# Second-type FFN of a twelve-part transformer program: two wide matmuls per product in place of three, all up products ahead of the down products

## The reference

```
def swiglu(x, w_gu, w_down):
    g, u = jnp.split(x @ w_gu, 2, axis=-1)
    return (jax.nn.silu(g) * u) @ w_down

h = x + 0.5 * swiglu(rmsnorm_2(x, g[0]), w_ffn_gu[layer, 0], w_ffn_down[layer, 0])
xn = rmsnorm_2(h, g[1])
...                                  # one of three mixers on xn, added to h
h = h + 0.5 * swiglu(rmsnorm_2(h, g[2]), w_ffn_gu[layer, 1], w_ffn_down[layer, 1])
gate = jax.nn.sigmoid(rmsnorm_2(h, g[3]) @ w_ple_gate[layer])
x = h + gate * (p[layer] @ w_ple_proj[layer])
```

## Time and profile before

| | us |
|---|---|
| median of three runs | 3411.81 (3410.1 to 3412.32) |
| span of the profiled execution, first to last instruction | 3410.7 |
| PE busy | 3235.4 (95%) |
| DVE busy | 2467.3 (72%) |
| ACT busy | 1768.7 (52%) |
| mean granted clock of TensorE, share of full | 0.968 |

### The profile page before, as it was taken

One profiled execution on the slowest core, in us unless ns is written; L12 is line 12 of the kernel. 1 busy time (PEld: TensorE's weight loads), 2 busy tenths in 40 slices (PEclk: granted clock), 3 DMA queues, 4 the chain that ended last, 5 costly groups with the idle time before them and its releaser, 6 DMA issues.

```text
span 3410.7 us, 64690 instructions
## 1 busy us (share of the span) xinstructions
PE 3235.4 (95%) x27210; PEld 3128.6 (92%) x27210; DVE 2467.3 (72%) x3720; ACT 1768.7 (52%) x2677; POOL 3.0 (0%) x6
## 2 busy tenths in 40 slices
PE   6899999999999999979999997999999999997999
PEld 6789899988989999879999987999989999997899
DVE  8987699887767766876676656667676667678666
ACT  4556444556554554665454535455455455457544
POOL 0000000000000000000000000000000000000000
PEclk8899999989999999989999998999999999998999
DMA  8455488434546555425555533555543555552453
GB/s 303 141 175 192 151 317 305 152 129 142 185 155 217 171 187 188 153 92 184 188 178 190 187 116 124 190 180 185 188 147 127 186 184 183 190 173 88 153 190 125
DMA packets 164353, 597.95 MB, mean 175 GB/s; under 512 B 18240, under 2 KB 18272, under 8 KB 163936
## 3 DMA queue, kind: packets, MB, share of 16 engines
q1 hardware_dynamic: 164064, 593.81, 51.5%
HBM read 592.69 MB, written 1.05 MB: 174 GB/s over the span
## 4 chain that ended last, share of the span: by engine, by line
PE 81%; DVE 12%; ACT 5%; issue 1%; DMA 1%; SPq 0%; DVEq 0%; ACTq 0%
PE ps L458 26%; PE ps L460 25%; PE ps L459 25%; DVE wlo L418 3%; ACT whi L406 1%; DVE fa L1527 1%; PE ps L1119 1%; ACT hh L1723 1%; DVE hl L1761 1%; PE ps L1235 0%; DVE land L533 0%; DMA land<-w_ada 0%; DVE fa L2225 0%; DMA land<-w_in 0%; DVE tmps L1801 0%
## 5 line engine op out<-in xcount | busy, mean ns | idle before, releaser
L458 PE MATMUL ps<-hh,whi 128*128 128x256 f32 x5472 | 1546.9, 283 | 46.7 <-DVE hl L732 20.5
L459 PE MATMUL ps<-hl,whi 128*128 128x256 f32 x5472 | 1536.2, 281 | 0.0
L460 PE MATMUL ps<-hh,wlo 128*128 128x256 f32 x5472 | 1535.6, 281 | 0.0
L418 DVE TENSOR_TENSOR wlo<-land,whi 128x1024 fp32r<-128x1024 f32 (+1 forms) x1032 | 1216.5, 1217 | 192.3 <-ACT whi L406 191.4
L406 ACT ACTIVATE whi<-land 128x1024 fp32r<-128x1024 f32 (+1 forms) x1032 | 1029.2, 1046 | 150.4 <-PE ps L460 136.1
L458 PEld LDWEIGHTS ps<-hh,whi 128*128 128x128 f32 x5472 | 1037.3, 190 | 56.2 <-issue 36.1
L459 PEld LDWEIGHTS ps<-hl,whi 128*128 128x128 f32 x5472 | 1037.3, 190 | 0.7
L460 PEld LDWEIGHTS ps<-hh,wlo 128*128 128x128 f32 x5472 | 1036.7, 189 | 0.0
L458 PE MATMUL ps<-ra,whi 128*128 128x256 f32 (+1 forms) x2416 | 684.3, 283 | 21.6 <-DVE ra L1435 11.9
L459 PE MATMUL ps<-ra,whi 128*128 128x256 f32 (+1 forms) x2416 | 679.4, 281 | 0.0
L460 PE MATMUL ps<-ra,wlo 128*128 128x256 f32 (+1 forms) x2416 | 679.1, 281 | 0.0
(11 more groups left out here) (416 smaller groups left out, 2441.9 us busy)
## 6 DMA issues: line engine op xcount, KB each, us to landing
land<-w_gu SPq DMA_DIRECT2D x352, 512.0 KB, 3.5
land<-w_dn SPq DMA_DIRECT2D x176, 512.0 KB, 3.5
land<-w_in SPq DMA_DIRECT2D x136, 512.0 KB, 3.8
land<-w_ada SPq DMA_DIRECT2D x96, 512.0 KB, 3.7
land<-w_up SPq DMA_DIRECT2D x88, 512.0 KB, 4.2
land<-hg_in SPq DMA_DIRECT2D x64, 512.0 KB, 3.5
land<-w_down SPq DMA_DIRECT2D x44, 512.0 KB, 4.5
land<-ple_gate SPq DMA_DIRECT2D x32, 512.0 KB, 3.5
```

The lines of the kernel that those rows point to most:

```text
L418: dve.tensor_tensor(w.lo, g.slot(n), w.hi.bitcast(F32), ALU.subtract).then_inc(*D_("w_lo", n))
L458: pe.matmul(out, w.hi, x.hi, start=first, stop=False, skip_group_check=skip)
L459: pe.matmul(out, w.hi, x.lo, start=False, stop=False, skip_group_check=skip)
L460: return pe.matmul(out, w.lo, x.hi, start=False, stop=last, skip_group_check=skip)
```

## The change

Only the second-type FFN changes, besides the layout of buffers. The hi and lo parts of h and of the inner activation now lie in one buffer at a fixed distance (class `Operand`, with `both` for the two), so that a unit is two matmuls (`wide`): w.lo·x.hi over 256 columns into the left half of a bank, and w.hi on both parts of x over 512 columns into both halves. A product so takes a whole bank, and its left and right halves have to be added by whoever reads it.

- The 22 up products come first, each in two banks (`up_banks`: 0 and 1, 2 and 3, 4 and 5, 6 and 7 in turn), and their activations are all kept (`y`, 128x11264, hi and lo). Then the down product is made chunk by chunk of the output, bank m for chunk m, over all 22 inner chunks; the down weights are laid out in that order on the host (`halved`).
- Per j, ScalarE copies the right halves of both banks (`up_right`, new, 128x512), VectorE adds them to the left halves (`up_read`, new, 128x512) and then multiplies by the factor (`up`). The splits of two tiles stand between these steps.
- The additions to x are made during the down product, two banks at a time, each in two instructions (left, right), and with them the next stage's hi parts, squares and lo parts for chunks 0 to 5; chunk 6 is added at tile 19, and chunk 7 (part 4) after the last tile.
- `norm2_tensor` stays after j = 1.

The diff, cut to the second-type FFN:

```diff
+def wide(pe, ps, w, x, first, last):
+    pe.matmul(ps[:, 0:T], w.lo, x.hi, start=first, stop=False, skip_group_check=True)
+    return pe.matmul(v2(ps), w.hi, x.both, start=False, stop=last, skip_group_check=True)
...
+    if before[0] == "h":
+        added_halves_vector(g, dve, before, ffn_number(before), 4)
+        for k in halves(3):
+            rest_vector(g, dve, st, which, k)
+        pair_vector(g, dve, st, 3)
+        reduced_vector(g, dve, st)
+        return
...
+def up_banks(j):
+    return 2 * (j % 4), 2 * (j % 4) + 1
+def up_tensor(g, pe, st, i, j, ready=None):
+    a, b = up_banks(j)
+    n = [take_tensor(g, pe, "w_gu", half) for half in halves(i * 22 + j)]
+    for bank in (a, b):
+        pe.wait_ge(*W(*g.banks.use(bank, "up_read", st, j)))
+    for k, c in [(k, c) for k in range(8) for c in range(2)] if ready else [(k, c) for c in range(2) for k in range(8)]:
+        if ready and c == 0:
+            pe.wait_ge(*W(*ready[k]))
+        mm = wide(pe, g.ps[(a, b)[c]], g.weights(n[c])[:, k * 128:(k + 1) * 128], g.h.chunk(k), k == 0, k == 7)
+        if k == 7:
+            mm.then_inc(*D_("tile", n[c]))
+def down_banks_tensor(g, pe, st, i, y):
+    for t in range(NF):
+        n = take_tensor(g, pe, "w_dn", down_tile(i, t))
+        for b in range(8):
+            m, k = divmod(8 * t + b, NF)
+            if m == 0:
+                pe.wait_ge(*W("inner", st, k))
+            if k == 0:
+                pe.wait_ge(*W(*g.banks.use(m, *(("acc_read", st, 3) if m == 6 else ("x", AFTER[st], m // 2)))))
+            mm = wide(pe, g.ps[m], g.weights(n)[:, b * 128:(b + 1) * 128], y.chunk(k), k == 0, k == NF - 1)
+            if b == 7:
+                mm.then_inc(*D_("tile", n))
+            elif k == NF - 1 and m in (1, 3, 5, 6):
+                mm.then_inc(*D_("acc", st, m))
...
 def second_ffn_tensor(g, pe, st, i):
     second_norm_tensor(g, pe, st)
-    ffn_tensor(g, pe, st, "w_gu", i * 22, "w_dn", i * 11, inner_pairs(g.ra2))
+    y = inner_operand(g)
+    up_tensor(g, pe, st, i, 0, chunks("h", st))
+    for p in range(NF // 2):
+        for j in halves(p):
+            if j:
+                up_tensor(g, pe, st, i, j)
+        if p == 0:
+            norm2_tensor(g, pe, st)
+    down_banks_tensor(g, pe, st, i, y)
...
+        act.wait_ge(*W("tile", n))
+        act.activation(v2(c), halves_of_banks(g, up_banks(j)[0], 2)[:, :, 1, :], ACT.Copy).then_inc(*D_("up_right", st, j))
+        if j > 1:
+            catch_up_scalar(g, act, n, 1)
+        act.wait_ge(*W("up", st, j))
         act.activation(b[:, 0:T], a[:, 0:T], ACT.Silu).then_inc(*D_("silu", st, j))
+        if j > 1:
+            catch_up_scalar(g, act, n)
         act.wait_ge(*W("prod", st, j))
...
+    for t in range(NF):
+        take_scalar(g, act, "w_dn", down_tile(i, t))
+        if t in (6, 12, 17):
+            q = (6, 12, 17).index(t)
+            gained_scalar(g, act, nx, next_norm(i), q)
+            square_scalar(g, act, nx, q)
...
 def second_ffn_vector(g, dve, st, i):
     D_, W = g.m.done, g.m.when
     second_norm_vector(g, dve, st, i // 2 * 4 + i % 2 * 2)
-    R = inner_pairs(g.ra2)
+    y, nx = inner_operand(g), AFTER[st]
     r = g.small[:, T:2 * T]
     for j in range(NF):
         p = j // 2
-        if j != 1:
-            take_vector(g, dve, "w_gu", *halves(i * 22 + j))
         if j == 0:
+            take_vector(g, dve, "w_gu", *halves(i * 22))
             take_vector(g, dve, "w_gu", *halves(i * 22 + 1))
             factor_vector(g, dve, st)
+        elif j > 1:
+            take_vector(g, dve, "w_gu", *halves(i * 22 + j), behind=2)
         n = g.index["w_gu", 2 * (i * 22 + j) + 1]
         if j == 10 and st[1] == "b":
-            low_vector(g, dve, ("p", "pl" + st[2]), ple_operand(g), g.fa2[:, 4096:4608], ("p_hi", "pl" + st[2]))
-        a, b = g.t(j % 2), g.t(2 + j % 2)
-        dve.wait_ge(*W("tile", n))
-        dve.tensor_tensor(v2(a), v2(g.ps[4 + j % 3][:, :]), bc2(r), ALU.mult).then_inc(*D_("up_read", st, j))
+            low_vector(g, dve, ("p", "pl" + st[2]), ple_operand(g), per_layer(g), ("p_hi", "pl" + st[2]))
+        a, b, c = g.t(j % 2), g.t(2 + j % 2), g.t(4 + j % 2)
+        dve.wait_ge(*W("up_right", st, j))
+        dve.tensor_tensor(v2(a), halves_of_banks(g, up_banks(j)[0], 2)[:, :, 0, :], v2(c), ALU.add).then_inc(
+            *D_("up_read", st, j))
+        dve.wait_ge(*W("up_read", st, j))
+        dve.tensor_tensor(v2(a), v2(a), bc2(r), ALU.mult).then_inc(*D_("up", st, j))
+        if j > 1:
+            catch_up_vector(g, dve, n, 1)
         dve.wait_ge(*W("silu", st, j))
-        dve.wait_ge(*W("up_read", st, j))
+        dve.wait_ge(*W("up", st, j))
         dve.tensor_tensor(b[:, T:2 * T], b[:, 0:T], a[:, T:2 * T], ALU.mult).then_inc(*D_("prod", st, j))
-        low_vector(g, dve, ("inner", st, j), R[p % 3].chunk(j % 2), b[:, T:2 * T], ("inner_hi", st, j))
-        if j % 2 and p:
-            take_vector(g, dve, "w_dn", *halves(i * 11 + p - 1))
-    take_vector(g, dve, "w_dn", *halves(i * 11 + NF // 2 - 1))
+        if j > 1:
+            catch_up_vector(g, dve, n)
+        low_vector(g, dve, ("inner", st, j), y.chunk(j), b[:, T:2 * T], ("inner_hi", st, j))
+    for t in range(NF):
+        take_vector(g, dve, "w_dn", down_tile(i, t))
+        if t in (5, 11, 16):
+            added_halves_vector(g, dve, st, i, (5, 11, 16).index(t))
+        elif t in (6, 12, 17):
+            q = (6, 12, 17).index(t)
+            for k in halves(q):
+                rest_vector(g, dve, nx, next_norm(i), k)
+            if q:
+                pair_vector(g, dve, nx, q)
+        elif t == 19:
+            added_halves_vector(g, dve, st, i, 3)
+def added_halves_vector(g, dve, st, i, part):
+    first, n = ((0, 2), (2, 2), (4, 2), (6, 1), (7, 1))[part]
+    s, banks = g.x[:, first * T:(first + n) * T].rearrange("p (b t) -> p b t", b=n), halves_of_banks(g, first, n)
+    dve.wait_ge(*W(*acc_ready(g, st, i, part)))
+    dve.scalar_tensor_tensor(s, banks[:, :, 0, :], 0.5, s, ALU.mult, ALU.add).then_inc(*D_("acc_left", st, part))
+    dve.wait_ge(*W("acc_left", st, part))
+    dve.scalar_tensor_tensor(s, banks[:, :, 1, :], 0.5, s, ALU.mult, ALU.add).then_inc(
+        *(D_("acc_read", st, part) if part == 3 else D_("x", AFTER[st], min(part, 3))))
```

More of the change, by code:

```diff
@@ L1750, in second_norm_scalar @@
         act.preload_act_table_set(NORM_TABLE)
-    for p in range(4):
+    for p in (3,) if before[0] == "h" else range(4):
         gained_scalar(g, act, st, which, p)
@@ L1817, in norm2_tensor @@
     D_, W = g.m.done, g.m.when
+    bank = MISC
     pe.wait_ge(*W("x_reduced", st))
-    pe.wait_ge(*W(*g.banks.use(MISC, "newton", st, 0)))
-    pe.matmul(g.ps[MISC][:, 0:T], g.C("ones", 0, 128), g.t(9)[:, 0:T], start=True, stop=True).then_inc(*D_("sumsq", st))
+    pe.wait_ge(*W(*g.banks.use(bank, "newton", st, 0)))
+    pe.matmul(g.ps[bank][:, 0:T], g.C("ones", 0, 128), g.t(9)[:, 0:T], start=True, stop=True).then_inc(*D_("sumsq", st))
 def factor_scalar(g, act, st):
@@ L3187, in ko, with halved @@
         return np.stack([np.ascontiguousarray(w[a:a + 128]) for w in ws for a in range(0, 2816, 128)])
+    def halved(ws):
+        tiles = []
+        for w in ws:
+            blocks = [w[k * 128:(k + 1) * 128, m * 128:(m + 1) * 128] for m in range(8) for k in range(NF)]
+            tiles += [np.concatenate(blocks[a:a + 8], 1) for a in range(0, 176, 8)]
+        return np.stack(tiles)
     def mixed(ws, plan, by_rows):
@@ L3243, in ride, with second_ffn_tiles @@
                 done += 1
+    def second_ffn_tiles(i):
+        for p in range(NF // 2):
+            pairs("w_gu", *[i * 22 + j for j in halves(p)])
+        add("w_dn", *[down_tile(i, t) for t in range(NF)])
     def ffn_tiles(up, up0, down, dn0):
```

88 lines of the change are left out of this document (53 added, 35 removed).

## The result

The changed kernel takes 3433.29 us (median of 4 runs, 3432.57 to 3434.38) against 3411.88 us of the kernel before in the same comparison: ratio 1.0063, 95% interval 1.0049 to 1.0077. It is slower by some 21 us, which the four runs tell clearly from no change. The profiled execution has a span of 3431.9 us, 21.2 us more than before. 3428 was forecast; sign and size came out, but the working did not in four places: a term that was counted at nothing is a gain of 14 us, another is five times larger than forecast, one place of loss was missing, and the mixers, counted as unchanged, were 5 us shorter in the two traces. They offset each other.

The account below looks back on a forecast made before the run. TensorE, busy 95% of the span, was taken as the bound. Terms 0 + 4.8 + 9.6 + 9.6 - 7.9 = +16.1 us on a span of 3410.7 gave 3428 us (+0.47%), with a range of 3406 to 3440.

Parts of the forecast that it names:

- Two matmuls for three: TensorE's units in the eight FFNs: 350.0 ns before and after, the 4224 removed matmuls hidden or free, 0 us.
- a unit shorter than 349 ns: Sign that the prediction is wrong, in the FFNs' units: it would move everything, each 1 ns being 4.2 us.
- rival of a price per instruction: Each removed FFN matmul gives back a fixed price; at 10.0 ns 3386 us; chance 0.12, shared with a mixer gain.
- fixed 2.5 ns per matmul: Rival from the skill page: the 4224 removed FFN matmuls give back 10.6 us, ending near 3417 us; chance 0.04.
- ScalarE and VectorE in the up products: Per j in the up products, the added copy and addition lie under TensorE's 5.60 us: 0 us.
- The start of each FFN: VectorE's backlog after the factor makes TensorE wait 0.6 us before j = 4 in eight FFNs: +4.8 us, bounds 0 and 12.
- The start after a mixer: At four hb starts TensorE waits for the fourth addition to free bank 0: +9.6 us, and +9.6 us of lower clock.
- Inside the mixers: From ha into a mixer nothing is won, and VectorE time freed there is counted at 0.
- The end of each FFN: From hb to pl, waits for the first chunk of h and the sum of squares go, at four places: -7.9 us.
- the third: Rival: VectorE's chain per j in the up products stretches beyond 5.60 us; 3474 us at 0.3 us excess; chance 0.06.
- The first: Rival: the backlog at FFN starts costs nothing and the gap after a mixer no clock; 3414 us; chance 0.19.

Follow-up runs that it names:

- e7: Changed kernel with the weight's second part also multiplied with both parts of x, so two 512-column matmuls to a unit: 3911.4 us.
- e9: Changed kernel with each tile's eight 256-column matmuls first, then its eight of 512, in up products behind j = 0: 3447.22 us.
- e2: Changed kernel, but from j = 1 on TensorE waits for an up product's second weight tile only after the first tile's eight units: 3406.39 us.
- e3: Changed kernel, but up products after a mixer use banks 4-5, 2-3, 0-1, 6-7, so the first avoids the bank of the fourth addition: 3412.33 us.
- e8: Changed kernel with the edits of e2 and e3, and tile 8 of each second-type FFN split during j = 1, one j earlier: 3382.45 us.

## Why the prediction was right, and where it was not

- **Two matmuls for three, forecast 0, measured -14.1 us.** The failed step is "116.7 + 233.3 = 350.0 ns after". Both numbers are right, each beside its like (e7, e9), and they do not add where the lengths alternate: 346.67 ns. The bounds on this term held the gain; the value did not. By the prediction's own sign ("a unit shorter than 349 ns") this part was wrong. The rival of a price per instruction is not what happened either: at its 3.33 ns it would have to be there in e9, whose instruction count is the same, and it is not. The Trainium skill's fixed 2.5 ns per matmul (page "TensorE: Matmul & The Clock Gate", section "Wait — 56ns, not 53.3ns?") comes near in size, 10.6 for 14.1 us, but e9 speaks against it as the cause in the same way.
- **ScalarE and VectorE in the up products, forecast 0, measured 0.** Inside the stream there are no gaps; the copy took 595 ns and the addition 691.
- **The start of each FFN, forecast +4.8, measured +17.7 and +7.8 of clock.** The chain on VectorE was right to a tenth of a microsecond (the first split ends 0.6 us late). The failed step is "TensorE wants it after j = 2 and j = 3": that is so of the first tile, but TensorE wants both, and the second split ends 1.5 us later. The prediction priced the wait as `proj_tensor` of the kernel before would meet it; `up_tensor` of the changed kernel takes both tiles at once, as the diff shows, and e2 brings the wait down to 0.48 us. The term's upper bound, 12, was too low as well. The clock behind so short a gap was not counted, on the strength of one gap of 2.3 us without it (and the gap here); after the change five of eight had it.

```profile
983.03 0.36 PE L458 MATMUL ps<-hh,whi 128*128 128x256 f32 x1 [2.34 <-DVE hl L732]
```

- **From pl into the next ha, not in the forecast, measured +6.4.** The same two-tile wait, before j = 1, in three FFNs (e2 takes it away). It was missed because only the start after a mixer and the backlog behind the factor were followed, and the wait for two tiles was not compared with that of the kernel before.
- **The start after a mixer, forecast +19.2 (9.6 and 9.6 of clock), measured +16.4.** Gap (4.9 us forecast, 4.98 measured) and cause (e3) were as described. The clock was at 0.50 for 3.4 us and then full, which is 1.7 us in hb0, where 2.4 were taken from two gaps that had a second slower stretch behind them. e3 against the changed kernel gives 16.5 for the same stretch.
- **Inside the mixers, forecast 0, measured -4.8.** Nearly all of it is in layer 3. There, 42 us behind the mixer's mark, the kernel before waits 2.67 us, and from the end of that wait the granted clock is 0.50 up to 3063.5 us, for 6.8 us in all; the changed kernel waits 1.40 us and keeps the full clock, as both do at the same place in layer 0, which has the same mixer. Every run of this document with the changed kernel or an edit of it has 1.40 us in layer 3, and only one trace of the kernel before exists. Whether the freed VectorE did this (the prediction counted that at 0) or whether it differs between executions of the kernel before is not shown.
- **The end of each FFN, forecast -7.9, worked out from e8 as -9.2.** No gap is left between hb and pl, as said. It was not tried apart.
- **The rivals.** There is no gap before every j, so the third fell. The first (3414: the backlog costs nothing and the gap no clock) fell too, since both cost time.

So the total was near because errors met. Not seen were +20.7 before j = 4 and +6.4 behind pl; counted too high was the start after a mixer, by 2.8; not seen as gains were the units' 14.1, the mixers' 4.8 and 1.3 of the ends. That is +4.1, and 21.2 stand against 16.1. So it took luck to come this near: without the wait for the second tile, which the prediction did not see, the kernel is at 3406 (e2), 22 us under the forecast.
